# Attention's products in a new order, the mixer norm's squares added on VectorE, and the second block of weights loaded earlier, in a hybrid decoder step

## The reference

```python
def rmsnorm(x, g):
    y = x * rsqrt(mean(x * x, axis=-1) + EPS) * g
def cross_attn(q, mem_k, mem_v):
    s = einsum('bthd,bmhd->bhtm', q, mem_k) * XA_DIM ** -0.5
    p = softmax(s, axis=-1)
    o = einsum('bhtm,bmhd->bthd', p, mem_v)
def trunk(x, ...):
    for i in range(2):
        h = rmsnorm(x, norm_mix[i])
        z = h @ w_in[i]
        mix = conv_mixer(z...) if i == 0 else retention_mixer(z...)
        xa = cross_attn(q_x, mem_ks[i], mem_vs[i])
        x = x + concatenate([mix, xa]) @ w_out[i]
        x = x + hier_moe(rmsnorm(x, norm_ffn[i]), ...)
    return rmsnorm(x, final_norm), ...
```

## Time and profile before

| | |
|---|---|
| median of 3 runs | 1214.72 us |
| the profiled execution's own time | 1214.7 us |
| its span, first to last instruction | 1212.4 us |
| PE busy | 1162.0 us, 96% |
| DVE, ACT, POOL busy | 356.8, 155.0, 11.8 us |
| moved by DMA | 364.59 MB, mean 301 GB/s |
| mean granted TensorE clock | 0.991 |

### The profile page before, as it was taken

How to read it: one execution, slowest core, us unless ns; L and a number is a source line. 1 busy time by engine, 2 the same in 40 slices (tenths; PEclk the granted TensorE clock), 3 DMA queues, 4 the chain that set the end, 5 groups by cost and what they waited for, 6 DMA issues and landing times.

```text
span 1212.4 us, 13805 instructions
## 1 busy us (share of the span) xinstructions
PE 1162.0 (96%) x5942; PEld 684.5 (56%) x5942; DVE 356.8 (29%) x871; ACT 155.0 (13%) x363; POOL 11.8 (1%) x22
## 2 busy tenths in 40 slices
PE   7999999999999999989999999999999999998885
PEld 6567776677554343436655656466677763443333
DVE  5221223212213131344224243433401022342225
ACT  2000002112211111120201011011200031110002
POOL 0000000000000000000000000000000000000000
PEclk9999999999999999999999999999999999999989
DMA  9953336833988999999255657382997559999993
GB/s 371 428 218 139 138 132 281 358 139 134 418 349 351 428 426 429 430 425 420 95 205 202 240 191 304 138 333 110 411 424 286 192 189 396 429 428 426 428 428 160
DMA packets 29743, 364.59 MB, mean 301 GB/s; under 512 B 3456, under 2 KB 3600, under 8 KB 7024
## 3 DMA queue, kind: packets, MB, share of 16 engines
q1 hardware_dynamic: 26784, 339.87, 68.6%
q10 hardware_dynamic: 1712, 19.17, 3.8%
q0 software_dynamic: 1184, 4.63, 1.0%
HBM read 339.34 MB, written 24.32 MB: 300 GB/s over the span
## 4 chain that ended last, share of the span: by engine, by line
PE 86%; DMA 11%; DVE 1%; issue 1%; ACT 1%; POOL 0%; SPq 0%; DVEq 0%; ACTq 0%
PE bank L866 23%; PE bank L568 13%; DMA ring<-in_gu 11%; PE bank L679 6%; PE bank L654 5%; PE bank L950 5%; PE bank L457 5%; PE bank L451 4%; PE bank L722 4%; PE bank L691 3%; PE bank L921 1%; PE bank L516 1%; PE bank L503 1%; PE bank L1031 1%; PE bank L471 1%; PE bank L1012 1%
## 5 line engine op out<-in xcount | busy, mean ns | idle before, releaser
L866 PE MATMUL bank<-hT,ring 128*128 128x288 f32 x1088 | 268.2, 407 | 0.9 <-issue 0.9
L866 PEld LDWEIGHTS bank<-hT,ring 128*128 128x128 f32 x1088 | 205.7, 190 | 66.9 <-issue 11.9
L568 PE MATMUL bank<-arena,ring 128*128 128x288 f32 x592 | 146.3, 406 | 0.0
L568 PEld LDWEIGHTS bank<-arena,ring 128*128 128x128 f32 x592 | 111.2, 190 | 29.6
L679 PE MATMUL bank<-ring,arena 128*32 128x512 f32 x896 | 106.1, 614 | 15.1 <-DMA ring<-in_gu 15.1
L654 PE MATMUL bank<-arena 128*128 128x512 f32 (+1 forms) x192 | 95.9, 625 | 0.2 <-ACT arena L1196 0.2
L679 PEld LDWEIGHTS bank<-ring,arena 128*32 128x32 f32 x896 | 28.4, 111 | 87.0 <-issue 73.4
L722 PE MATMUL bank<-arena 128*128 128x288 f32 x256 | 68.9, 413 | 3.2 <-issue 2.8
L1514 DVE TENSOR_TENSOR xT<-xT,bank 128x288 f32<-128x288 f32 x128 | 58.1, 454 | 30.4 <-PE bank L722 26.7
L654 PEld LDWEIGHTS bank<-arena 128*128 128x128 f32 (+1 forms) x192 | 31.1, 187 | 63.4 <-issue 62.3
L722 PEld LDWEIGHTS bank<-arena 128*128 128x128 f32 x256 | 46.2, 190 | 23.7 <-issue 7.6
(11 more groups left out here) (259 smaller groups left out, 900.0 us busy)
## 6 DMA issues: line engine op xcount, KB each, us to landing
ring<-in_gu SPq DMA_DIRECT2D x56, 2048.0 KB, 19.4
ring<-in_dn SPq DMA_DIRECT2D x29, 2048.0 KB, 16.9
ring<-in_rin SPq DMA_DIRECT2D x14, 2048.0 KB, 13.5
ring<-in_cin SPq DMA_DIRECT2D x8, 2048.0 KB, 27.4
ring<-in_kc SPq DMA_DIRECT2D x8, 2048.0 KB, 7.9
ring<-in_vc SPq DMA_DIRECT2D x8, 2048.0 KB, 10.3
ring<-in_st SPq DMA_DIRECT2D x8, 2048.0 KB, 10.3
out_rs<-ring ACTq DMA_DIRECT2D x8, 2048.0 KB, 8.3
```

Of the source, the lines that this page charges most:

```text
L568: mm = pe.matmul(bank[1 + o % 4][:, 0:T], w[k], cat[:, k, :], start=(k == 0), stop=(k == kt - 1))
L866: mm = pe.matmul(outs[o], w[:, o, k, :], src[:, k, :], start=(k == 0), stop=(k == KD - 1))
```

## The change

- In `attention`, `pv(0)` moves ahead of `turn(2)`, `decode_values(0)` from behind `pv(1)` to behind `scores(4)`, and `decode_values(1)` from behind `scores(7)` to behind `scores(6)`. Every `turn` from 3 on then has a `pv`, a `decode_values`, or other blocks between itself and the last `scores`.
- `mix1` joins `COLLECTED`: DVE adds six of its blocks of squares, and PE's part shrinks from 8 matmuls to 2; it now stands behind product o = 1 of the projection and not o = 0. Waits on the count `squares_added` are renumbered.
- The loads of `xT` and `cst` are issued behind the load of `kv0` block 1 and not ahead of it.
- At the end, the second quarter of the last output is copied by ACT, between its fourth and fifth square, and not by DVE.

```diff
-        COLLECTED = {"mem": 0, "mix0": 1}
+        COLLECTED = {"mem": 0, "mix0": 1, "mix1": 3}
...
-                if n == 0:
+                if n == 1:
                     sp.dma_start(xT, a["xT"]).then_inc(S("x_in"), 16)
                     sp.dma_start(cst[:, 2 * P:NCC], a["cst"][:, 2 * P:NCC]).then_inc(S("const_in"), 16)
...
                 turn(1)
                 scores(3)
+                pv(0)
                 turn(2)
-                pv(0)
                 turn(3)
                 scores(4)
+                decode_values(0)
                 turn(4)
                 scores(5)
                 pv(1)
-                decode_values(0)
                 turn(5)
                 scores(6)
+                decode_values(1)
                 turn(6)
                 scores(7)
-                decode_values(1)
                 pv(2)
                 turn(7)
...
-                pe.wait_ge(S("squares_added"), i + 3)
+                pe.wait_ge(S("squares_added"), 2 * i + 3)
...
                         if o == 6 and L == 1 and i == PACKS - 1:
-                            pe.wait_ge(S("y_out_d"), 2 * PACKS + 1)
+                            pe.wait_ge(S("y_out_a"), 2 * PACKS + 1)
...
-                    pe.wait_ge(S("squares_added"), 5)
+                    pe.wait_ge(S("squares_added"), 6)
...
-                    if src is early and o == 0:
+                    if src is early and o == 1:
                         norm_sum("mix1", T)
...
                     for k in range(KD):
+                        if k == 4:
+                            act.wait_ge(S("y_sum"), 4 * PACKS + 1)
+                            act.activation(yo[:, 768:1024], bank[5][:, 0:256], ACT.Copy).then_inc(S("y_out_a"), 1)
                         act.wait_ge(S("y_added"), KD * PACKS + KD * (PACKS - 1) + k + 1)
...
                         dve.tensor_copy(yo[:, 512:768], bank[6][:, 0:256]).then_inc(S("y_out_d"), 1)
-                        dve.wait_ge(S("y_sum"), 4 * PACKS + 1)
-                        dve.tensor_copy(yo[:, 768:1024], bank[5][:, 0:256]).then_inc(S("y_out_d"), 1)
...
             for k in range(KD):
                 dve.tensor_scalar(early[:, k, :], xT[:, k, :], G("mix1")[:, k:k + 1], None, ALU.mult) \
                    .then_inc(S("early"), 1)
+            for k in range(KD):
+                add_square("mix1", T, k)
             V_(dve.memset(qm_, 0.0))
```

## The result

The changed kernel took 1206.69 us (median of 4 runs, 1206.16 to 1207.23), the kernel before 1214.57 us in the same comparison: ratio 0.9930, 95% interval 0.9918 to 0.9941, that is 7.2 to 10.0 us less. Four launches lay far above all others (two of the kernel before, at 1364 and 2438 us, one of head_only, at 1744, one of the changed kernel, at 1355), and every median, mean and ratio here leaves them out. The profiled execution of the changed kernel took 1206.16 us, with a span of 1204.4 us.

What follows compares the result with a forecast made beforehand. PE, busy 96% of the span, was taken to bound the kernel. Gains of 1.48 + 2.8 + 2.1 + 2.91 = 9.3 us from 1214.7 us gave 1205.4 us, range 1203.6 to 1208.9.

Steps and rivals of the forecast that it cites:

- the sum: Whole kernel: 1.48 + 2.8 + 2.1 + 2.91 = 9.3 us gained against the profiled 1214.7 us.
- step 1: Kernel start: `kv0` block 1 lands 5.1 us sooner, so PE's wait at 21.96 goes; gain 1.48 us.
- step 2: Attention: reordered blocks fill PE's idle time ahead of the turns; gain 2.8 us in layer 0, 2.1 in layer 1.
- The feared wait of `decode_values(0)`: Attention, layer 0: DVE's copy of job 2 fits by 0.2 us, or PE waits up to 0.9 us.
- Step 3: Mixer norm of layer 1: PE's part falls from 3.88 to 0.97 us; gain 2.91 us.
- The additions' margin: Mixer norm, layer 1: DVE's six additions end 3.2 us before PE asks for them.
- that of `hT`: Layer 1, ahead of `values(0)`: `hT` complete 1.4 us before PE needs it, where the margin was 5.2.
- Step 4: Kernel end: the copy fits ACT's idle time; gain nothing, bounds -0.4 to +0.4 us.
- Letting every microsecond through: Whole kernel: DMA-bound stretches move with PE, so all time won early reaches the end.
- the swallowing: Expert stages: full DMA stretches end when they did, so early gains vanish; 1214.7 us, chance 5%.
- The clock rival: Window 1100 to 1140: PE's clock stays at 1.2 GHz throughout, +21 us less 9.3, so 1226 us; chance 3%.
- The rival that the head stays: Kernel start: the "issue" wait hides something other than the weights' landing and remains; 1206.9 us, chance 8%.

Runs made afterwards that it cites:

- head_only: The kernel before with only the loads of `xT` and `cst` moved behind `kv0` block 1; median 1213.43 us, ratio 0.9987 (0.9975 to 1.0000).
- after_pv3: The changed kernel with layer 1's `pv(3)` ahead of `decode_values(3)` and the new tokens' transposes inside the output product; median 1206.40 us, ratio 0.9920.
- after_norm_o0: The changed kernel with the mixer norm's two matmuls back behind product o = 0; median 1207.36 us, ratio 0.9934 (0.9916 to 0.9951).
- tail_only: The kernel before with only the last output's quarter copied by ACT; median 1216.14 us, ratio 1.0002 (0.9991 to 1.0014).
- attention_only: The kernel before with only the new order of attention's blocks; median 1210.63 us, ratio 0.9962 (0.9943 to 0.9981).

## Why the prediction came out as it did

The forecast was 1205.4 us, with 1203.6 to 1208.9 as its range. The medians were 1206.7, 1206.4 and 1205.9 us, and the kernel before was at 1214.6 beside the first, 1215.5 and 1215.1 beside the others, so the difference, 9.3 us by the sum, came out at 7.9, 9.1 and 9.2 (8.5, 10.5 and 9.5 by the ratios). That the sum was met this closely is in part luck: step 1 was 0.4 us too high and step 2 was 0.4 us too low. Point by point:

- *Step 1* was mis-sized: "Gain: 1.48 us". The mechanism held, since the second weights landed 5.1 us sooner and the gap went. The step took PE's arrival at 21.96 for granted, which rested on the fastest L442 of all fourteen profiles; on average the wait is shorter and the part is worth about 1.05 us. The move of `xT` and `cst` cost nothing: DVE's additions followed at 25.90 in the changed kernel, right behind the memory norm.
- *Step 2, layer 0*: 2.8 forecast, 3.12 measured in every profile with the new order. The idle times were 2.88 of it. The rest is in the joints: a `pv` followed by a `turn` costs 1.72 us where one followed by `decode_values` costs 1.82, and two turns side by side 0.43. The feared wait of `decode_values(0)` for DVE's copy did not come.
- *Step 2, layer 1*: 2.1 forecast, 2.2 measured. The wait moved to the last block of values, 0.87 us and not 0.7, as PE came 0.3 us earlier than I had it. The first block was in time. And the output product's weights are next in line, as after_pv3 showed.
- *Step 3*: 2.91 forecast, 2.92 measured. The additions' margin (3.2 us) came out at 3.4 and that of `hT` (1.4) at 1.35. The 0.6 us that the old place would have cost are 0.84 by after_norm_o0.
- *Step 4*: nothing forecast, nothing that the runs could tell from nothing (tail_only: a gain between -1.7 and +1.1 us).
- *Letting every microsecond through* was right for DMA. The lead of 9.2 us at the output product stood unchanged at the routing. PE's waits for expert weights went from 15.1 to 13.7 us. That is 0.4 us more than the 1 us by which the forecast let them move, but away from the swallowing, and well inside what the profiles show (14.2 to 15.8 us in the five without the whole change, 13.5 to 16.6 in the nine with it). What it passed over is the routing: there the clock took 1.6 us back in the profiled execution, so what failed in that execution is not a term of the sum but the silence on the clock outside the last stage.
- *The clock rival* had put it in the window from 1100 to 1140, at 21 us. The lower level stood there for 6.8 us before and 6.8 us after, and it decided nothing. The rule that the rival named, from the Trainium skill ("TensorE: Matmul & The Clock Gate", section on HAM oscillation), is that waits for the next data send the work behind them back to the throttled rate. The trace agrees with it only in the last stage, where PE waits for weights: there the clock fell in all fourteen profiles, for 6.8 to 13.7 us, and the stage took 207.4 to 208.9 us with 6.8 and 207.8 to 208.9 with 13.7, so no price is to be seen. In the routing PE waits for no weights, and no longer than 1.2 us for anything; the price there was 0 to 2.5 us.
- The rival that the head stays, and the one that the expert stages swallow the gain, are refuted by head_only's trace and by attention_only's median.

## What to carry to other kernels

Where two engines pass work back and forth, write down for each block which earlier block it needs and how long the hand-over takes, and put a block at least that long in between; the gain is the sum of the idle times, and what is late next is often a load released by something else. A term taken from one trace is one draw: a wait that ends with a transfer shrinks when the work ahead of it runs late, so look at several profiles before pricing it. Judge small parts by the length of their own stretch in the trace and add them; a span of one execution (tail_only's) lay 4 us above that of the kernel before for reasons that its edit had not touched. A matmul that fills a wait and that nobody reads is not free: when the clock is low it can outlast the wait, as L642 did.

## What the runs showed of the hardware that was not expected

- TensorE's granted clock fell to the lower level in layer 1's routing in ten of fourteen profiles, for 3.4 or 6.8 us, and in layer 0's in two, for 3.4 us. PE had waited 0.95 us just before the routing and ran narrow products in it, in the profiles with the fall as in those without. It cost between nothing and 2.5 us, depending on which matmuls fell into it.
- At the lower level the two instructions of a 128x512 float32 matmul (L642) took 2.05 us, against 1.10 at the full one.
- The work on the first 2 MB of weights and the memory (L442) took 8.6 to 10.2 us between executions, and did so with either order of loads.
